# Modulation sums on the partition halves: 512 outputs and 64 inputs to a half, and one two-column matmul for both

## The reference

```python
c_act = jax.nn.silu(c)                      # c: (1, 1024)
for l in range(2):
    mod = c_act @ ada_w[l] + ada_b[l]       # ada_w[l]: (1024, 6144)
    shift1, scale1, gate1, shift2, scale2, gate2 = split(mod, 6)
```

## Time and profile before

| | |
|---|---|
| median of 3 runs | 1102.77 us (1102.28 to 1104.78) |
| the profiled execution | 1105.96 us, of which its span 1104.1 us |
| TensorE's granted clock over the span | 0.994 |
| busy: PE, PEld, DVE, ACT, POOL | 1079.3, 1028.9, 821.9, 525.1, 30.3 us |
| pieces of the modulation | 96, of 512 KB each |

### The profile page before, as it was taken

How to read it: one execution, slowest core, us unless ns; L and a number is a source line. 1 busy time by engine, 2 the same in 40 slices (tenths; PEclk the granted TensorE clock), 3 DMA queues, 4 the chain that set the end, 5 groups by cost and what they waited for, 6 DMA issues and landing times.

```text
span 1104.1 us, 19435 instructions
## 1 busy us (share of the span) xinstructions
PE 1079.3 (98%) x8322; PEld 1028.9 (93%) x8322; DVE 821.9 (74%) x1096; ACT 525.1 (48%) x613; POOL 30.3 (3%) x54
## 2 busy tenths in 40 slices
PE   6999999999999999999999999999999999999998
PEld 5888799999998989979999999999898899999998
DVE  6878589887775899957887787869999576555552
ACT  4455665554434535545543433454455455344441
POOL 5100000000000010000000000000000000000000
PEclk9999999999999999999999999999999999999998
DMA  8666248888893554328698989846442375655551
GB/s 239 188 229 243 95 172 297 276 286 283 308 330 109 179 175 153 115 77 269 197 315 271 354 305 315 306 151 231 159 153 77 125 250 160 201 180 191 172 172 39
DMA packets 132845, 230.38 MB, mean 209 GB/s; under 512 B 6569, under 2 KB 60183, under 8 KB 132761
## 3 DMA queue, kind: packets, MB, share of 16 engines
q1 hardware_dynamic: 130404, 227.04, 61.3%
q0 software_dynamic: 1440, 0.85, 0.5%
q10 hardware_dynamic: 917, 1.27, 0.3%
HBM read 227.29 MB, written 1.06 MB: 207 GB/s over the span
## 4 chain that ended last, share of the span: by engine, by line
PE 71%; DVE 18%; ACT 6%; issue 3%; DMA 1%; SPq 0%; POOL 0%; DVEq 0%; POOLq 0%; ACTq 0%
PE mm L430 64%; DVE lo L1245 6%; DVE cacc L1335 5%; ACT hi L833 3%; PE mm L473 2%; PE pv L503 2%; ACT pB L912 1%; DVE ada_acc L1266 1%; DVE sB L1343 1%; DVE qk L1358 1%; PE pa L541 1%; DVE hf L1356 1%; DVE qk L1357 1%; DMA swap<-qk 1%; DMA xin<-in_x_dram 1%
## 5 line engine op out<-in xcount | busy, mean ns | idle before, releaser
L430 PE MATMUL mm<-act_hi,hi 128*128 128x256 f32 x1760 | 493.6, 284 | 2.5 <-ACT act_hi L901 1.8
L430 PE MATMUL mm<-act_hi,lo 128*128 128x256 f32 x1760 | 487.3, 280 | 0.0
L430 PE MATMUL mm<-act_lo,hi 128*128 128x256 f32 x1760 | 469.6, 280 | 0.0
L1245 DVE TENSOR_TENSOR lo<-raw,hi 128x2048 fp32r<-128x2048 f32 (+1 forms) x159 | 359.6, 2265 | 131.5 <-ACT hi L833 129.5
L833 ACT ACTIVATE hi<-raw 128x2048 fp32r<-128x2048 f32 (+1 forms) x160 | 302.1, 1892 | 232.0 <-PE mm L430 184.4
L430 PEld LDWEIGHTS mm<-act_hi,hi 128*128 128x128 f32 x1760 | 332.9, 189 | 6.4 <-issue 4.9
L430 PEld LDWEIGHTS mm<-act_hi,lo 128*128 128x128 f32 x1760 | 332.9, 189 | 0.4
L430 PEld LDWEIGHTS mm<-act_lo,hi 128*128 128x128 f32 x1760 | 322.2, 189 | 0.0
L430 PE MATMUL mm<-u_hi,hi 128*128 128x256 f32 x608 | 170.8, 281 | 0.0
L430 PE MATMUL mm<-u_lo,hi 128*128 128x256 f32 x608 | 169.8, 279 | 0.0
L430 PE MATMUL mm<-u_hi,lo 128*128 128x256 f32 x608 | 169.6, 279 | 0.0
(11 more groups left out here) (263 smaller groups left out, 950.3 us busy)
## 6 DMA issues: line engine op xcount, KB each, us to landing
ada_raw<-in_ada_w_dram SPq DMA_DIRECT2D x96, 512.0 KB, 5.7
raw<-in_w_ffn_in_dram SPq DMA_DIRECT2D x88, 512.0 KB, 5.4
raw<-in_w_in_dram SPq DMA_DIRECT2D x40, 1024.0 KB, 5.2
raw<-in_w_ffn_out_dram SPq DMA_DIRECT2D x20, 1024.0 KB, 6.2
raw<-in_w_up_dram SPq DMA_DIRECT2D x16, 1024.0 KB, 6.8
raw<-in_w_down_dram SPq DMA_DIRECT2D x16, 1024.0 KB, 7.7
raw<-in_w_out_dram SPq DMA_DIRECT2D x12, 1024.0 KB, 5.5
raw<-in_w_in_dram SPq DMA_DIRECT2D x16, 512.0 KB, 6.1
```

The costliest lines, as they stand in the source:

```text
L430: ins = pe.matmul(o, w[:, kk, fs], a[:, k, :], start=(k == 0 and i == 0 and f % 2 == 0), stop=(ends and i == len(pairs) - 1), skip_group_c ...
L1245: v(dve.tensor_tensor(lo[:, c % RING, 0:nk, :], raw[:, c % RING, 0:nk, :], hi[:, c % RING, 0:nk, :].bitcast(F32), ALU.subtract), "lo_done")
```

## The change

The accumulator is folded. The partitions are split into two halves of 64 (`ADA_B` = 2, `ADA_K` = 64). Half 0 works on outputs 0 to 511 of a group, half 1 on outputs 512 to 1023 (`ADA_F` = 512), and each takes the 128 inputs of a piece as two sets of 64. A piece is now loaded by two transfers of 256 KB, each into 64 partitions, and in each partition two rows of 2 KB. DVE takes a piece in two steps of 128 x 512 into an accumulator of 512 columns, the second of which needs the first. PE sums with 4 matmuls per group in the place of 8: the data are two columns (`blocks`), with ones for one half of the partitions each, and the two result columns stand 4 apart in the bank. The factors `ca` now need 16 columns, with 64 values of `c` in each half; `c` is therefore loaded twice by POOL, as 16 rows of 64 values into `adab`, and turned with the biases. It leaves the list of parameters, so that the two queues take other ones. Nothing else is moved: the pieces, sums and chunks stand in the same places on every engine.

```diff
@@ -58,6 +58,10 @@
 ADA_RING = 3
 ADA_ACCS = 2
 ADA_P = KD
+ADA_B = 2
+ADA_K = P // ADA_B
+ADA_F = ADA_W // ADA_B
+ADA_C = KD * ADA_B
 LAMBDA_INIT = [0.8 - 0.6 * float(np.exp(-0.3 * l)) for l in range(LAYERS)]
 MAGIC = 1.5 * 2.0 ** 23
 TWO_PI = (6.28125, 0.0019350051879882812, 3.0199157663446332e-07)
@@ -66,8 +70,10 @@
 
 
 C_ID, C_ONE = 0, P
-C_FREQ, C_ADD, C_UP = 2 * P, 2 * P + 1, 5 * P + 1
-C_ALL = 8 * P + 1
+C_FREQ, C_BLK = 2 * P, 2 * P + 1
+C_ADD = C_BLK + ADA_B
+C_UP = C_ADD + 3 * P
+C_ALL = C_UP + 3 * P
 
 
 def constants():
@@ -82,6 +88,7 @@
         if d < 2 * half:
             c[p, C_FREQ] = freq[d % half] * (-1.0 if d < half else 1.0)
     c[:, C_ONE:C_ONE + P] = 1.0
+    c[i, C_BLK + i // ADA_K] = 1.0
     tri = np.where(i[None, :] <= i[:, None], 0.0, -1e30)
     c[:, C_ADD:C_ADD + P] = tri
     c[:, C_ADD + 2 * P:C_ADD + 3 * P] = tri
@@ -196,7 +203,7 @@
 
     pack, srcs = {}, [
         ("g_mix_pre", t["g_mix_pre"][0], KD), ("g_mlstm", t["g_mlstm_out"][0], MH), ("g_mix_post", t["g_mix_post"][0], KD),
-        ("g_mlp_pre", t["g_mlp_pre"][0], KD), ("g_mlp_post", t["g_mlp_post"][0], KD), ("c", t["c_2"][0], KD),
+        ("g_mlp_pre", t["g_mlp_pre"][0], KD), ("g_mlp_post", t["g_mlp_post"][0], KD),
         ("final", t["final_g_2"], KD)]
     for l in range(LAYERS):
         srcs += [(("norm1", l), t["norm1_g_2"][l], KD), (("norm2", l), t["norm2_g_2"][l], KD), (("subln", l), t["subln_g_2"][l], 1),
@@ -244,7 +251,7 @@
         hi = sb("hi", [P, RING, CK, GF], F32R)
         lo = sb("lo", [P, RING, CK, GF], F32R)
         ada_raw = sb("ada_raw", [P, ADA_RING, ADA_W])
-        ada_acc = sb("ada_acc", [P, ADA_ACCS, ADA_W])
+        ada_acc = sb("ada_acc", [P, ADA_ACCS, ADA_F])
         cst = sb("cst", [P, C_ALL])
         x = sb("x", [P, KD, S])
         act_hi = sb("act_hi", [P, KD, S], F32R)
@@ -254,10 +261,10 @@
         rstd = sb("rstd", [P, 2, S])
         tabs = sb("tabs", [P, 2, 2 * S])
         parT = sb("parT", [P, NROW])
-        adabT = sb("adabT", [P, NMOD])
+        adabT = sb("adabT", [P, NMOD + ADA_C])
         modT = sb("modT", [P, NMOD])
         convw = sb("convw", [P, LAYERS * GT, TAPS])
-        ca = sb("ca", [P, 2, KD])
+        ca = sb("ca", [P, 2, ADA_C])
         cols = sb("cols", [P, 40])
         small = sb("small", [P, 24])
         nlam = sb("nlam", [P, LAYERS])
@@ -325,7 +332,9 @@
 
 
         outf = ada_raw[:, 0:2].rearrange("p a (t s) -> p (a t) s", s=S)
+        cT = adabT[:, NMOD:NMOD + ADA_C]
         ident = cst[:, C_ID:C_ID + P]
+        blocks = cst[:, C_BLK:C_BLK + ADA_B]
         ones = cst[:, C_ONE:C_ONE + P]
 
         def pcols(name):
@@ -375,7 +384,9 @@
                     if j >= ADA_RING:
                         sp.wait_ge(sem("ada_used"), j - ADA_RING + 1)
                     src = t["ada_w_2"][i // ADA_GROUPS, k * P:(k + 1) * P, i % ADA_GROUPS * ADA_W:(i % ADA_GROUPS + 1) * ADA_W]
-                    sp.dma_start(ada_raw[:, j % ADA_RING, :], src).then_inc(sem(f"ada_loaded{j % ADA_RING}"), 16)
+                    for b in range(ADA_B):
+                        sp.dma_start(ada_raw[b * ADA_K:(b + 1) * ADA_K, j % ADA_RING, :].rearrange("p (s f) -> p s f", s=ADA_B),
+                                     src[:, b * ADA_F:(b + 1) * ADA_F].rearrange("(s p) f -> p s f", p=ADA_K)).then_inc(sem(f"ada_loaded{j % ADA_RING}"), 16)
                     j += 1
                 if c >= RING:
                     if whole[c - RING]:
@@ -498,10 +509,9 @@
                     i = l * ADA_GROUPS + q + a
                     pe.wait_ge(sem("ada_used"), (i + 1) * ADA_P)
                     b = bank(2) if a == 0 else pv[2]
-                    for f in range(ADA_T):
-                        to = a * ADA_T + f
-                        ins = pe.matmul(b[:, to:to + 1], ada_acc[:, i % ADA_ACCS, f * P:(f + 1) * P], ones[:, 0:1], start=(to == 0), stop=True,
-                                        skip_group_check=True)
+                    for f in range(ADA_T // ADA_B):
+                        ins = pe.matmul(b[:, a * ADA_T + f:(a + 1) * ADA_T:ADA_T // ADA_B], ada_acc[:, i % ADA_ACCS, f * P:(f + 1) * P], blocks,
+                                        start=(a == 0 and f == 0), stop=True, skip_group_check=True)
                     if a == count - 1:
                         full(ins, 2)
 
@@ -596,10 +606,10 @@
             wait("positions_ready")
             full(pe.matmul(bank(1)[:], ones[0:1, :], posf[0:1, :], start=True, stop=True), 1)
             pe.wait_ge(sem("params_loaded"), 16 * (1 + len(srcs[::2])))
-            pe.wait_ge(sem("more_params_loaded"), 16 * len(srcs[1::2]))
+            pe.wait_ge(sem("more_params_loaded"), 16 * (len(srcs[1::2]) + ADA_B))
             b = bank(0)
             pe.transpose(b[:, 0:NROW], rows[0:NROW, :], ident[0:NROW, 0:NROW])
-            full(pe.transpose(b[:, P:P + NMOD], adab[0:NMOD, :], ident[0:NMOD, 0:NMOD]), 0)
+            full(pe.transpose(b[:, P:P + NMOD + ADA_C], adab[0:NMOD + ADA_C, :], ident[0:NMOD + ADA_C, 0:NMOD + ADA_C]), 0)
             bank("a")
             wait("sq_added")
             n("sq_ready", 4)
@@ -934,7 +944,7 @@
             high_of_norm(lambda k: hng[:, k, :], tiles=range(4, KD))
             split(groups[("in", 0)][1][0] + LEAD)
             wait("c_loaded")
-            a(act.activation(ca[:, 0, :], pcols("c"), ACT.Exp, scale=-1.0), "c_exp_ready")
+            a(act.activation(ca[:, 0, :], cT, ACT.Exp, scale=-1.0), "c_exp_ready")
             wait("lam_dots_ready")
             a(act.activation(lams[0:1, 4:8], lams[0:1, 0:4], ACT.Exp), "lam_exps_ready")
             split(groups[("in", 0)][1][1] + LEAD)
@@ -1183,6 +1193,8 @@
         def _(pool):
             p = Own(pool, sem, "pool_step")
 
+            for b in range(ADA_B):
+                pool.dma_start(adab[NMOD:NMOD + ADA_C, b * ADA_K:(b + 1) * ADA_K], t["c_2"][0].rearrange("(r p) -> r p", p=ADA_K)).then_inc(sem("more_params_loaded"), 16)
             for r, ap, tiles in list(pack.values())[1::2]:
                 pool.dma_start(rows[r:r + tiles, :], ap.rearrange("(r p) -> r p", p=P)).then_inc(sem("more_params_loaded"), 16)
             pool.wait_ge(sem("pos_loaded"), 32)
@@ -1257,13 +1269,16 @@
 
                 i = j // ADA_P
                 acc = ada_acc[:, i % ADA_ACCS, :]
-                dve.wait_ge(sem(f"ada_loaded{j % ADA_RING}"), 16 * (j // ADA_RING + 1))
+                dve.wait_ge(sem(f"ada_loaded{j % ADA_RING}"), 16 * ADA_B * (j // ADA_RING + 1))
                 k = j % ADA_P
-                w = ada_raw[:, j % ADA_RING, :]
-                if k == 0:
-                    link(dve.tensor_scalar(acc, w, ca[:, 1, 0:1], None, ALU.mult), "ada_used")
-                else:
-                    link(dve.scalar_tensor_tensor(out=acc, in0=w, scalar=ca[:, 1, k:k + 1], in1=acc, op0=ALU.mult, op1=ALU.add), "ada_used")
+                for r in range(ADA_B):
+                    w = ada_raw[:, j % ADA_RING, r * ADA_F:(r + 1) * ADA_F]
+                    done = "ada_used" if r == ADA_B - 1 else None
+                    if k == r == 0:
+                        link(dve.tensor_scalar(acc, w, ca[:, 1, 0:1], None, ALU.mult), done)
+                    else:
+                        at = k * ADA_B + r
+                        link(dve.scalar_tensor_tensor(out=acc, in0=w, scalar=ca[:, 1, at:at + 1], in1=acc, op0=ALU.mult, op1=ALU.add), done)
 
             def advance(c, pieces_first=False):
 
@@ -1389,7 +1404,7 @@
             v(dve.tensor_tensor(sq[:, 0, :], sq[:, 0, :], sq[:, 1, :], ALU.add), "sq_added")
             b = full(0)
             v(dve.tensor_copy(parT[:], b[:, 0:NROW]))
-            link(dve.tensor_copy(adabT[:], b[:, P:P + NMOD]), "bank0_free")
+            link(dve.tensor_copy(adabT[:], b[:, P:P + NMOD + ADA_C]), "bank0_free")
             dve.sem_inc(sem("c_loaded"), 1)
             def first_low(kk):
 
@@ -1433,7 +1448,7 @@
             wait("c_exp_ready")
             link(dve.tensor_scalar(ca[:, 0, :], ca[:, 0, :], 1.0, None, ALU.add))
             link(dve.reciprocal(ca[:, 0, :], ca[:, 0, :]))
-            link(dve.tensor_tensor(ca[:, 1, :], ca[:, 0, :], pcols("c"), ALU.mult), "c_ready")
+            link(dve.tensor_tensor(ca[:, 1, :], ca[:, 0, :], cT, ALU.mult), "c_ready")
 
             wait("lam_loaded", 16 * 4 * LAYERS)
             link(dve.tensor_tensor(lamp[0:1, :, :], lamr[0:1, :, 0, :], lamr[0:1, :, 1, :], ALU.mult))
```

## The result

The changed kernel takes 1181.85 us (median of 4 runs, 1170.05 to 1185.47) where the kernel before, run on the same chip, takes 1102.67 (1102.28 to 1104.78). The ratio is 1.0696, interval 1.0671 to 1.0722: **7.0% slower**, 79 us. The forecast was 1116.5, in a range of 1099 to 1138. The direction was right and the size far off. The profiled execution took 1185.47 us with a span of 1183.4, so it is 0.3% above the median.

The account below looks back on a forecast made before the run. PE, DVE's loop with ACT, and transfers were taken to run within some 10% of each other in the FFN stage. Sums -2.5, MLP transfers +1, FFN transfers +15: +13.5 us on 1102.8, rounded to 1116.5; range 1099 to 1138.

Parts of the forecast that it names:

- the transfers' term: Pieces' loads into 64 partitions get slower: +15 us in the FFN stage (ends 0, +35), +1 in the first block's MLP.
- What would show it: Signs listed beforehand, mostly for the FFN stage: DMA share 0.93 or more, under 280 GB/s, PE idle 10 to 20 us.
- The upper bound is the slow one: 2.7 us a piece. I take 2.3.: Transfer time of a changed piece: 2.3 us, between 1.6 and 2.7, where a piece took 1.5 before.
- The other 33.1 MB thus took 102 us: FFN stage: traffic other than the pieces took 102 of 173 us of transfer time, leaving 1.5 us a piece.
- the slow row: Earlier trace, 36 to 44 us: transfers into 8 partitions at 193 GB/s beside raw traffic, giving 2.7 us a piece.
- MLP term: First block's MLP, second half: transfers need 119 us in 115, with slack before it; +1 us, ends 0 and +12.
- the upper rival: Transfers cost 2.7 us a piece: +35 us in the FFN stage, up to +6 in the MLP, 1141 us; chance 0.15.
- The sums on PE: Each of 12 groups falls from 1.68 to 0.84 us: -2.5 us in MLP, -3.4 in FFN if PE-bound, 0 between stages.
- The pieces on DVE: Steps of 747 and some 480 ns, +25 us of DVE time; hidden in the MLP, +2 us net in the FFN stage.
- only the larger of this and the next term counts: FFN stage: DVE's +2 us and the transfers' +15 don't add, since a wait for transfers covers DVE's.
- The first rival: Transfers keep their price and the rest cancels: FFN +2, MLP -2.5, 1100 to 1103 us, likeliest 1102; chance 0.27.
- SP's issue and the start: SP's 96 more issues of 0.34 us and POOL's two more loads at the start are hidden: 0, end +1 for the start.

Follow-up runs that it names:

- experiment 1: Kernel before, each piece loaded by two transfers into 64 neighbouring partitions each, rows of 4 KB; 1168.38 us, ratio 1.0592.
- experiment 10: Kernel before with only its loads replaced by the change's (two into 64 neighbouring partitions, rows of 2 KB); 1177.73 us, ratio 1.067.
- experiment 3: Kernel before, each piece loaded by two transfers into all 128 partitions, half the columns each, rows of 2 KB; 1103.23 us, ratio 1.0002.
- experiment 7: Kernel before, each piece loaded by four transfers into 32 neighbouring partitions each, rows of 4 KB; 1180.96 us, ratio 1.0703.
- experiment 2: Kernel before, each piece loaded by two transfers into 64 partitions, one the even and one the odd, rows of 4 KB; 1103.39 us, ratio 1.0013.
- experiment 6: Kernel before with 4 of the 8 matmuls in each group of sums left out; 1097.3 us, ratio 0.9943.
- experiment 9: Kernel before with loads into neighbouring halves (rows of 4 KB) and DVE's two steps of 512 columns per piece; 1167.94 us, ratio 1.0563.
- experiment 5: The whole change with output halves interleaved on even and odd partitions, so each transfer reaches all partitions; 1110.98 us, ratio 1.0069 against the kernel before.
- experiment 8: The interleaved change with pieces moved from the FFN's first matrices to its second; 1119.01 us, ratio 1.0138 against the kernel before.

## Why the prediction was wrong

**The bound, right.** The views said that PE, DVE's loop and the transfers run within 10% of each other in the FFN stage, and that the transfers' term decides. It did, in both stages. Most of what "What would show it" named for the forecast came in the FFN stage: a share above 0.93, a rate below 280 GB/s, ACT's rounding waiting for DMA. One sign failed with the size: PE's idle time was to be 10 to 20 us there and nearly none in the MLP; it was 37 and 17.

**The step that failed** is the one that begins "The upper bound is the slow one: 2.7 us a piece. I take 2.3." Worked with the prediction's own sum, the price can be read from each stage, since both are full now. The FFN stage needed 173 us of the transfers; it takes 251 with 48 pieces, so a piece costs 78/48 = 1.6 us more than 1.5: **3.1 us**, if all that is added is charged to the pieces. The MLP needed 0.76 x 70 + 0.85 x 115 = 151 us; it takes 211 with 38 pieces, 60/38 = 1.6 us more: again 3.1. (The windows hold the packets of 45 of the 48 pieces and of 36 of the 38; counted so, it is 3.3 and 3.2.) Put in the place of 2.3, this gives 173 + 78 - 197 = +54 in the FFN stage, where the stage grew by 55.5, and 151 + 60 - 185 = +26 in the MLP, where it grew by 26. The price was read from these same stages, so this is no second measurement of it; what it shows is that one price serves both. One price was mis-sized, and nearly all that was missing follows from it. With it a term was put at nothing: the sum keeps the raw weights at the time that they took before ("The other 33.1 MB thus took 102 us"). The packets show otherwise. In experiment 1 a piece's own packets take 263 ns x 128 / 16 = 2.1 us of all engines in the FFN stage and 2.2 in the MLP, and the rest of its price is raw's packets lasting longer.

The same working on the experiments splits the 1.6 us. In experiment 1 the stages need 0.98 x 210 = 206 and 0.99 x 233 = 231 us, which makes 2.9 and 2.7 us a piece; in experiment 10 it is 3.1 and 3.0. So the neighbouring halves take the price, with all charged to the pieces, from 1.5 us to some 2.8, and the rows of 2 KB inside them add 0.2 to 0.3. My upper bound of 2.7 was nearly the price of the halves alone, and the rows were missing from it: I had priced their length from the earlier trace rows, raw chunks over all partitions, where experiment 3 confirms that it costs nothing. The two properties had been priced apart, and by these runs they don't act apart.

The choice within the bounds was wrong too. I let speak against the earlier trace rows, though both are four transfers of 32 KB, and a few that small say little of a stream of transfers of 256 KB. They are also of another kind: they carry `swap` from `qk`, from one place of the on-chip memory to another, in packets of 1 KB, where the pieces come from DRAM. And I took part of the slow row as "waiting behind raw packets" and cut the price for it, when that row was the one with the traffic that the pieces have beside them.

**The Trainium skill** was right where I overruled it. SBUF — State Buffer, "Door 1: The DMA port swizzle", has partitions 0 to 63 reach half of the 16 ports, and 32 neighbouring ones the same 8 ports as the 64 that hold them. Experiments 1 and 7 bear that out (+65 and +77 us), and experiment 2 does from the other side, since every second partition reaches all ports by the same table and costs nothing. No trace shows the ports themselves. Its figure of 196 GB/s gave an estimate of 2.7 us a piece, and experiment 1 has 2.7 to 2.9, with the slower raw packets in it; the 1140 us that I made of it were too few because my MLP term was short (below) and the rows of 2 KB were at no price. Its sentence under "Can I just issue two DMAs to hit both halves?", that the only way to all ports is one transfer over all 128 partitions, is not borne out: experiment 2 has two transfers into 64 partitions each and loses nothing. That two transfers to the two halves don't make up for each other is what experiment 1 shows.

**The MLP term** ("I take +1, ends 0 and +12") fell with the price. At 2.3 us the stage needs 151 + 38 x 0.8 = 181 us of its 185, which just fits. At 2.7 it needs 197, the end of +12; the upper rival took only half of that ("up to +6"). At the 2.9 of experiment 1 it needs 204, and there the stage grew by 24 us (215.6 for 191.3).

**The sums on PE, right.** A group takes 0.81 us, from 151.45 to 152.26 in the changed kernel, for 0.84 predicted; a matmul with two columns costs what one with one column does. Saved over the whole kernel: 6.6 us (experiment 6), between the 5.9 of seven groups and the 8.4 with groups between stages. In the changed kernel none of it can be seen, as predicted for the FFN stage and against the -2.5 for the MLP.

**The pieces on DVE, durations right, effect half right.** Steps of 752 and 482 ns for 747 and 480 predicted, +24.3 us for +25. That a wait for transfers covers DVE's loop ("only the larger of this and the next term counts") is what experiment 9 shows. Its own effect was undersized: +2 us net was predicted for the FFN stage if the transfers kept their price, and experiment 5 has +7.0 (208.3 for 201.3). PE waits 7.3 us there, not 5, and its granted clock over the stage is 0.97 for 0.99, some 4 us that were not counted; less the 3.4 saved, that is about the 7. The first rival, priced at 1102, would thus have come out at 1111, nearly where the forecast lay for another reason.

**SP's issue and the start, right.** Experiment 2 shows the longer and doubled issue at no cost. The matmul that turns the parameters is at 13.08 us instead of 12.41, and the first product's matmul starts at 16.69, before the 17.38 of the kernel before: POOL's two loads delay nothing.

**Open.** Why the length of the rows matters only inside halves, why raw packets last longer beside the pieces of a neighbouring half, and how much of the 8 us of experiment 8 is the order of SP's queue.

## What to carry to other kernels

When an edit changes which partitions a transfer writes, check first that it still reaches all of them or a spread set; 64 spread partitions were as good as 128 here, 64 neighbouring ones cost nearly twice the transfer time here, and half or more of what was added fell on the traffic beside them. Lay a fold out interleaved (p mod 2) rather than in blocks, so that its loads stay whole. And when a rule and one small row disagree over the term that decides, keep the rule's case as the likelier one unless the row has the size and the company of the new transfers.

## What was unexpected of the hardware

A neighbouring quarter is hardly worse than a neighbouring half (+77 against +65 us), and an odd or even half isn't worse than the whole (+0.4 us by the medians, -0.3 to +3.2 by the interval of the ratio). Pieces that reach a half make the raw packets beside them last a third longer and more (65 ns for 49, 124 for 88). The length of a row matters only together with the reach: 2 KB for 4 KB costs 0.2 us over all partitions (experiment 3) and about 10 us inside halves (experiment 10 against 9). And an issue on SP takes 0.6 us for a transfer into 64 partitions, in either layout, where it takes 0.34 for one into 128, 0.43 for one into 128 with half the columns (experiment 3) and 0.42 for one into 32 (experiment 7). In the changed kernel:

```profile
L388 SPq DMA_DIRECT2D ada_raw<-in_ada_w_dram x192: 595/606/2141, 50.2 to 791.1; - x192
```
